# Key, value, output gate and z tiles of the first projection as pairs of half-size products

## What is computed

```python
hn = _rmsnorm(x, pre_g).astype(x.dtype)
proj = jnp.einsum('bld,de->ble', hn, w_in).astype(F32)          # 1024 -> 7176 features
q, k, v, og, ig, fg, z, xr, gr = _split(proj, EVEN_SPLITS)      # 1024 each; ig, fg: 4 each
kh = _heads(k, M_HEADS) * (M_DK ** -0.5)
li = (ig + b_i.astype(F32)).transpose(0, 2, 1)
lf = jax.nn.log_sigmoid(fg + b_f.astype(F32)).transpose(0, 2, 1)
...
hm = jax.nn.sigmoid(og) * hm
hm = _head_norm(hm, m_norm_g, M_HEADS) * jax.nn.silu(z)
```

## Time and profile before

| | us |
|---|---|
| median of 3 runs | 2317.79 (2316.91 to 2320.01) |
| profiled execution | 2318.86 |
| its span, first to last instruction | 2317.1 |
| mean granted clock of TensorE | 0.974 |
| VectorE busy / ScalarE busy / GpSimd busy | 1080.8 / 764.4 / 284.2 |

### The profile page before, as it was taken

One profiled execution on the slowest core, in us unless ns is written; L12 is line 12 of the kernel. 1 busy time (PEld: TensorE's weight loads), 2 busy tenths in 40 slices (PEclk: granted clock), 3 DMA queues, 4 the chain that ended last, 5 costly groups with the idle time before them and its releaser, 6 DMA issues. The chain is left out here.

```text
span 2317.1 us, 32021 instructions
## 1 busy us (share of the span) xinstructions
PE 2188.5 (94%) x12374; PEld 1898.7 (82%) x12374; DVE 1080.8 (47%) x1935; ACT 764.4 (33%) x1406; POOL 284.2 (12%) x287
## 2 busy tenths in 40 slices
PE   5999999999999799999986999999999799999998
PEld 4999999999999567767756999999999466666665
DVE  5455612121112565565535656755666654444442
ACT  5455512112221433333225444321232432222222
POOL 3010000000000111121113000000000332322232
PEclk8999999999999799999997999999999899999999
DMA  2122134333332644344313233344332544444442
GB/s 98 60 72 69 49 93 123 93 111 102 94 101 75 204 128 131 117 134 142 110 47 121 84 92 90 119 151 127 107 95 84 195 160 140 161 146 154 148 132 64
DMA packets 204453, 261.89 MB, mean 113 GB/s; under 512 B 47584, under 2 KB 151264, under 8 KB 202288
## 3 DMA queue, kind: packets, MB, share of 16 engines
q1 hardware_dynamic: 204336, 260.30, 35.7%
HBM read 170.29 MB, written 89.97 MB: 112 GB/s over the span
## 5 line engine op out<-in xcount | busy, mean ns | idle before, releaser
L361 PE MATMUL pa_ps<-a_XT_hi,pa_w_hi 128*128 128x358 f32 x1344 | 301.7, 333 | 0.3 <-PEq L196 0.3
L361 PE MATMUL pa_ps<-a_XT_hi,pa_w_lo 128*128 128x358 f32 x1344 | 293.9, 327 | 0.0
L361 PE MATMUL pa_ps<-a_XT_lo,pa_w_hi 128*128 128x358 f32 x1344 | 293.3, 326 | 0.0
L361 PEld LDWEIGHTS pa_ps<-a_XT_hi,pa_w_hi 128*128 128x128 f32 x1344 | 233.0, 189 | 5.9 <-issue 0.6
L361 PEld LDWEIGHTS pa_ps<-a_XT_hi,pa_w_lo 128*128 128x128 f32 x1344 | 232.2, 189 | 0.0
L361 PEld LDWEIGHTS pa_ps<-a_XT_lo,pa_w_hi 128*128 128x128 f32 x1344 | 231.6, 189 | 0.0
L345 DVE TENSOR_TENSOR pa_w_lo<-pa_w_raw,pa_w_hi 128x1024 fp32r<-128x1024 f32 x57 | 70.7, 1240 | 318.1 <-ACT pa_w_hi L341 315.8
L1833 DVE TENSOR_TENSOR pc_stage<-pc_ps,pc_stage 128x536 f32<-128x536 f32 x110 | 77.0, 712 | 105.0 <-PE pc_ps L1802 91.5
L954 PE MATMUL mc_ps<-mc_wout_hi,mc_mix_hi 128*128 128x512 f32 x288 | 118.9, 413 | 2.3 <-POOL mc_mix_lo L2753 1.4
L954 PE MATMUL ma_ps<-ma_wout_hi,ma_mix_hi 128*128 128x512 f32 x288 | 120.8, 419 | 0.0
L954 PE MATMUL ma_ps<-ma_wout_lo,ma_mix_hi 128*128 128x512 f32 x288 | 115.1, 400 | 0.0
(11 more groups left out here) (451 smaller groups left out, 4746.3 us busy)
## 6 DMA issues: line engine op xcount, KB each, us to landing
pa_w_raw<-in_w_a SPq DMA_DIRECT2D x57, 512.0 KB, 4.3
pc_w_raw<-in_w_c SPq DMA_DIRECT2D x49, 512.0 KB, 4.6
scr_c<-pc_stage SPq DMA_DIRECT2D x48, 512.0 KB, 3.2
scr_a<-pa_stage SPq DMA_DIRECT2D x40, 512.0 KB, 3.2
ma_hin<-scr_a SPq DMA_DIRECT2D x32, 512.0 KB, 3.7
mc_hin<-scr_c SPq DMA_DIRECT2D x32, 512.0 KB, 3.7
mc_sample_state<-in_s SPq DMA_DIRECT2D x32, 512.0 KB, 4.6
out_s_s<-mc_sample_state SPq DMA_DIRECT2D x32, 512.0 KB, 2.7
```

The costliest lines, as they stand in the source:

```text
L361: ins = pe.matmul(self.ps[:, 3 * s + t, 0:TC], w[:, k, :], x[:, k, t * TC:(t + 1) * TC], start=(k == 0 and j == 0), stop=(k == KT - 1 and ...
```

## The change

The k, v, og and z tiles of the first projection (32 tiles, from tile 25, `A_PAIRS0`, on) are made as 16 pairs with `HalfProducts`. The class moves ahead of `stage_project_a`, takes the number of its first tile, the scratch for the sums and the write semaphores as arguments, and takes in the methods that stood in `stage_project_c` (token sums, copies, additions). The q tiles stay as they are, written out instead of looped. Beside them run now: the gate rows (ScalarE at tile 0, VectorE at tiles 0 and 1, TensorE before tile 4, ScalarE's reading after tile 3), the token sums (tiles 2 to 5), and the weight sums of the first pair. The scaling of k, the sigmoid of og and z and the multiplication of z work in place on the staging tiles once the additions are through. The buffers of the channel recurrence are given back before those of the half products are taken; the gate rows lie in the space of the output weights, whose four loads are issued in pairs 1 to 4. In the second projection the calls are put in new places, with the same operations in the same order.

```diff
+A_PAIRS0 = 25
 # SP
+                for k in range(8):
+                    n, s = A_QKV0 + k, (1 + k) % 2
+                    if k < 6:
+                        G.load(sp, n + 2, s)
+                    else:
+                        HP.load(sp, 0, s)
+                    spill(stage_ready, k + 1, s, k // 2, k % 2)
...
+                sp.wait_ge(rows_ready, 1)
+                sp.dma_start(out_m, m_out[:]).then_inc(finished, 16)
+                for p in range(NPAIR):
+                    kind, h = kind_of(p)
+                    if p + 1 < NPAIR:
+                        for s in range(2):
+                            HP.load(sp, p + 1, s)
+                    if 1 <= p <= w_out.tiles // 2:
+                        sp.wait_ge(rows_turned, 1)
+                        sp.wait_ge(HP.t_ready, 1)
+                        w_out.load(sp, p - 1)
+                    for m in range(2):
+                        if kind == "v":
+                            spill(HP.added, HP.ready(p)[m], m, h, 4 + m)
+                        else:
+                            spill(final[m], tile_count(p), m, h, 2 * (1 + p // 4) + m)
 # ScalarE
+                for k in range(8):
+                    if k == 7:
+                        HP.split_lower_hi(act, 0)
+                        HP.split_upper_hi(act, 0)
+                    q_tile(k)
+                    if k == 0:
+                        gate_rows_act(act)
+                    if k == 2:
+                        act.wait_ge(lru_spilled, 32 * 8)
+                    if 2 <= k < 2 + KH:
+                        for i in range(2 * k - 4, 2 * k - 2):
+                            HP.t_his(act, i)
+                    if k == 3:
+                        gate_rows_act_out(act)
+                    if k == 6:
+                        HP.split_sums_hi(act, 0)
+                HP.t3_his(act)
...
+                    if kind == "k":
+                        act.activation(flat[m][:, 0:T], flat[m][:, 0:T], ACT.Copy, scale=0.0625).then_inc(final[m], 1)
+                    elif kind == "og":
+                        act.activation(flat[m][:, 0:T], flat[m][:, 0:T], ACT.Sigmoid).then_inc(final[m], 1)
                     else:
+                        act.wait_ge(z_read, 2 * h + m)
+                        act.activation(z_sig, flat[m][:, 0:T], ACT.Sigmoid).then_inc(sigmoid_ready, 1)
+                for p in range(NPAIR):
+                    more = p + 1 < NPAIR
+                    HP.copies(act, p, upper, lower)
+                    if more:
+                        HP.split_upper_hi(act, p + 1)
+                        HP.split_sums_hi(act, p + 1)
+                    finish(p, 0)
+                    if more:
+                        HP.split_lower_hi(act, p + 1)
+                    finish(p, 1)
 # VectorE
+                for k in range(6):
+                    G.split_lo(dve, A_QKV0 + 2 + k, (1 + k) % 2)
+                    if k < 2:
+                        gate_rows_dve(dve, k)
+                    else:
+                        for i in range(2 * k - 4, 2 * k - 2):
+                            HP.t_sums(dve, i)
+                            HP.t_lows(dve, i)
+                HP.sum_weights(dve, 0)
+                HP.t3_sum(dve, 0)
+                HP.t3_sum(dve, 1)
+                HP.split_sums_lo(dve, 0)
+                HP.split_lower_lo(dve, 0)
+                HP.split_upper_lo(dve, 0)
+                HP.t3_lows(dve)
...
+                for p in range(NPAIR):
+                    if p > 12:
+                        z_gate(p - 1, 1)
+                    HP.sums_of(dve, p, upper, lower, p + 1 < NPAIR, (lambda: z_gate(p, 0)) if p >= 12 else (lambda: None))
+                z_gate(NPAIR - 1, 1)
 # TensorE
+                for k in range(2, 8):
+                    if k == 4:
+                        gate_rows_pe(pe)
+                    n = A_QKV0 + k
+                    G.products(pe, n, (1 + k) % 2, n // 2, {})
+                pe.wait_ge(G.psum_free[1], A_PAIRS0 // 2)
+                pe.wait_ge(toks_read, 1)
+                for p in range(NPAIR):
+                    HP.products(pe, p)
```

The methods that these calls reach, as far as they are not those of the class before:

```diff
+    def copies(self, act, p, upper, lower):
+        if p == 0:
+            act.wait_ge(self.spilled[1], 32 * self.before)
+            self.copy(act, p, 5, lower[1])
+            self.copy(act, p, 4, lower[0])
+        act.wait_ge(self.spilled[0], 32 * (self.before + p))
+        self.copy(act, p, 1, upper[0])
+    def t_his(self, act, i):
+        k = i // 2
+        for m, (u, x) in enumerate(self.t_made(i)):
+            act.wait_ge(self.t_sum, 3 * k + i % 2 + m + 1)
+            act.activation(self.t_hi[u][:, k, :], x, ACT.Copy).then_inc(self.t_hi_ready, 1)
```

More of the change, by code:

```diff
@@ L414, in stage_project_a @@
         e_last = a.sb("pa_e_last", [4, 17])
+        temps = a.sb("pa_t_temps", [P, 3, HC])
+        lru = ExitStack()
+        la = make_alloc(nc, lru)
+        xe_p = la.sb("pa_xe_p", [P, 3 + NP_TOK])
+        xe_s = la.sb("pa_xe_s", [P, NSEQ, 3 + SLEN])
+        xc = la.sb("pa_xc", [P, TP])
+        gr_e = la.sb("pa_gate_r", [P, TP])
+        gi_e = la.sb("pa_gate_i", [P, TP])
+        av = la.sb("pa_decay", [P, T])
+        tv = la.sb("pa_tanh", [P, T])
+        lv = la.sb("pa_log", [P, T])
+        hv = la.sb("pa_h", [P, T])
+        silu = la.sb("pa_silu", [P, 3, TC])
+        sig = la.sb("pa_sigmoid", [P, 3, TC])
+        silu_f = silu[:].rearrange("p a b -> p (a b)")
+        lout = la.sb("pa_lru_out", [P, T])
+        lru_w = la.sb("pa_lru_w", [P, 2, P])
+        conv0 = la.sb("pa_conv0", [P, 8, NSEQ, 3])
+        h0 = la.sb("pa_h0", [P, 8, NSEQ])
+        lru.close()
+        room = w_out.rows[:].rearrange("p t d -> p (t d)")
+        gates, rows = room[:, 0:TP], room[:, TP:TP + T]
+        xf, ab, lf, bb, mm = (room[0:4, TP + (1 + k) * T:TP + (2 + k) * T] for k in range(5))
         sem = S.a.sem
@@ L445, in stage_project_a @@
         rows_turned = sem("pa_rows_turned")
+        toks_read = sem("pa_row_columns_read")
+        final = [sem(f"pa_{x}_tile_ready") for x in ("upper", "lower")]
+        z_read = sem("pa_z_sigmoid_read")
+        HP = HalfProducts(S, G, a, a, "pa", A_PAIRS0, tuple(temps[:, k, :] for k in range(3)) + (room[:, 7 * T + 2:7 * T + 2 + HC],), spilled, 4)
+        z_sig = temps[:].rearrange("p k t -> p (k t)")[:, 0:T]
         PROMPT = slice(0, NP_TOK)
@@ L457, in seqs, with kind_of, tile_count, halves @@
             return buf[:, NP_TOK:NP_TOK + NSEQ * SLEN].rearrange("p (s t) -> p s t", t=SLEN)
-        groups = ("q", "k", "v", "og", "z")
-        xf, ab, lf, bb, mm = (x[0:4, 0:T] for x in (gr_e, gi_e, av, tv, lv))
+        NPAIR = 16
+        def kind_of(p):
+            return ("k", "v", "og", "z")[p // 4], p % 4
+        def tile_count(p):
+            return p + 1 if p < 4 else p - 3
+        def halves(buf):
+            return [buf[:, m * HC:(m + 1) * HC].rearrange("p (a b) -> p a b", b=HC // 2) for m in range(2)]
+        upper, lower = halves(flat[0]), halves(flat[1])
         li = gates[0:4, 0:T]
@@ L496, in gate_rows_dve_0 @@
         def gate_rows_dve_0(dve, link):
-            link(dve.memset(rows[:], 0.0))
+            link(dve.memset(rows, 0.0))
             link(dve.memset(m_prev[:], 0.0))
@@ L699, in _ @@
-                for g in range(len(groups)):
-                    last = g == len(groups) - 1
-                    if g == 0:
-                        for d in range(2):
-                            tile(g, 0, d, False, True)
-                    with act.Fori(1 if g == 0 else 0, 3 if last else 4) as h:
-                        for d in range(2):
-                            tile(g, h, d, False, False)
-                    if last:
-                        for d in range(2):
-                            tile(g, 3, d, True, False)
-                    if g == 0:
-                        gate_rows_act(act)
-                    if g == 3:
-                        gate_rows_act_out(act)
+                    if k >= 2:
+                        act.wait_ge(spilled[s], 32 * (k // 2))
@@ L2012, in _ @@
                     g, h, d = head_of(p)
-                    if p == 0:
-                        act.wait_ge(spilled[1], 32 * 8)
-                        HP.copy(act, p, 5, lower[1])
-                        HP.copy(act, p, 4, lower[0])
-                    act.wait_ge(spilled[0], 32 * (8 + p))
-                    HP.copy(act, p, 1, upper[0])
+                    HP.copies(act, p, upper, lower)
                     if p + 1 < NPAIR:
@@ L2144, in _ @@
                 HP.split_upper_lo(dve, 0)
-                for k in range(KH):
-                    t3_low(k)
-                    if k + 2 < KH:
-                        t3_sum(k + 2)
+                HP.t3_lows(dve)
                 def gate(p, m, x):
```

567 lines of the change are left out of this document (254 added, 313 removed).

## The result

| | before | after |
|---|---|---|
| median, us (4 runs each) | 2318.9 (2316.91 to 2320.13) | 2282.0 (2279.99 to 2283.07) |
| profiled execution / its span | 2318.86 / 2317.1 | 2283.07 / 2281.3 |
| mean granted clock | 0.974 | 0.969 |

The ratio is 0.984 with a 95% interval of 0.982 to 0.985: faster by 37 us. Forecast were 2278, with a range of 2271 to 2288.

The account below looks back on a forecast made before the run. The prediction took the changed tiles to be bound by TensorE's matmuls alone. Its terms, -46.4 + 1.1 + 3.7 + 1.7 = -39.9 us, took 2318.86 to 2279.0, so a median of 2278 us, range 2271 to 2288.

Parts of the forecast that it names:

- The matmuls: Key, value, output gate and z tiles: 379.7 us removed, 16 pairs at 333.3 us added, a gain of 46.4 us.
- The end of the stage: Last product's read to next stage's first transfer: 7.09 us instead of 6.03, so +1.1 us for one more addition.
- The stall: Hand-over to the first pair: TensorE waits 3.7 us for split weight sums, 3.0 to 6.8 with the load's landing.
- The low clock: Behind the hand-over gap the granted clock drops to 0.50 for 3.4 us, costing 1.7 us.
- rival 2: Longer hand-over: load meets the query tile's write, takes 7.4 us, low clock lasts 6.8 us; 2283 us, chance 0.17.
- The query tiles: They take over gate rows and token sums at zero cost, with 4.6 us of cover behind the gate rows.
- Within the pairs: First projection's pairs cost nothing beyond the second layer's; tightest cover 5.8 us, for the copy of product 1.
- the twin: Second layer's projection, already run as pairs of seven half-size products at 123.7 ns a matmul; most prices come from it.
- The second layer: Its code is only rearranged, so its cost was put at zero.
- the sum: All terms together, -39.9 us against the profiled execution of 2318.86 us, giving 2279.0 us.
- Rival 1: Shorter hand-over: the load lands early and the clock is not lowered; 2275.5 us, chance 0.12.
- Rival 4: Slower than before: matmul pace follows the number of weight loads instead of the columns; 2386 us, chance 0.03.

## Why the prediction was right, and where it was not

1. **The matmuls.** Forecast 333.3 us for 16 pairs at 123.7 ns. Measured from the first product to the reading of the last: 711.28 - 376.62 = 334.7, less 1.6 for the clock = 333.0, which the run with the early load, without a low clock, shows by itself. The run with eight products prices a matmul at 123.7 ns by itself. Right, and shown.
2. **The end of the stage.** Forecast 7.09 us; measured 718.47 - 711.28 = 7.19.
3. **The stall.** Forecast 3.7; measured 3.91. The chain was the one worked out (load, weight sums, two token sums, low part): taking the load out of it removed the stall, and taking the token sums out of it removed 2.7 us. Step by step from the end of tile 6 (360.84): load on its way at +2.6 us, landed at +7.0, weight sums at +9.5, token sums at +13.8, low part done at +15.5, as forecast. What the prediction did not see is the second wait right behind it, that of the fifth product for ScalarE's copy: it shows only when the first is shortened alone.
4. **The low clock.** Forecast 1.7, half of a drop of 3.4 us; measured a drop of 3.4 us, and 1.6 us less in the pairs where it is gone. The size rested on one row. In the run with 8 late copies and in that with 210 columns, at stalls of 4.0 and 3.6 us, the drop was rival 2's 6.8.
5. **The query tiles.** Forecast zero with 4.6 us of cover behind the gate rows; measured zero, with 4.5 us (307.0 to 311.5), and the added clears were paid from exactly there. VectorE was through with the last token sums 11.7 us into their tile (348.97 to 360.66); 11.8 were forecast.
6. **Within the pairs.** Forecast zero, with 5.8 us as the tightest cover; measured zero. The 5.8 us hold for the last three pairs (about 6 us). But the middle pairs have 8.1, and the tightest place is pair 1 with 4.3, which the prediction missed: in the twin that copy had ended 4.3 us into the pair, here the write of pair 0 holds it to 7.6. It cost nothing, so the zero was right, but in pair 1 with less room than stated. Taking 5.8 for every pair made the forecast for 14 copies twice too large.
7. **The second layer.** Costed at zero, and wrong: +1.0 in its norm and projection and +2.5 in its mixing, both repeated in the second traces. The 3 us of range for drops in the mixing stages covered it, and drops they are, but the prediction took them for scatter around zero. Against the 2279.0 of the sum the profiled execution took 2283.07: of these 4.1 us 3.5 are the second layer, 0.7 the two stages around the first projection, and the first projection is 0.1 better than forecast.
8. **Rival 1 and 2** (2275.5 and 2283). The measured time lies near rival 2's, but neither of its mechanisms happened: the stall was 3.9 and the low clock 3.4 us. The time alone would have told the wrong story.
9. **Rival 4.** The pace by weight loads. Not at 268 columns, but a floor exists: it begins near 230 to 241 columns (an estimate), at 106 to 111 ns, well under the 138.8 from which the change would have lost. The Trainium skill (TensorE: Matmul & The Clock Gate, Back-to-back issue gap), from which the prediction had 81 ns for 128 columns and 131 ns for 512, is not borne out here: the line through both gives 82 ns for 134 columns and 99 for 268, estimates, and 134 columns took 212.8 ns at clock 0.50, 106 by halving, and 268 took 123.7. Nor does its N / 2.4 + 2.5, which it calls the gap of an isolated matmul, describe this stream: it gives 90 ns for 210 columns and 114 for 268, estimates, where 111.2 and 123.7 were measured.

## What to carry to other kernels

Where a stretch is bound by TensorE alone and a twin of the new form already runs in the kernel, the twin's pace times the count gives the gain to a microsecond; what is left to work out is the hand-over, instruction by instruction on each queue, and the gaps' cost in clock on top of their length. Compare stages, not whole times: the stage that was changed repeated within 0.1 us here, while unchanged stages behind it moved by 2.5. Cutting matmuls into smaller ones pays only while they are above the floor, some 230 to 240 columns for this data by the estimate above; the scheme applied a second time would fall under it. Mend a stall at the first link of its chain, for a shortcut in the middle may only uncover the next wait.

## What the runs showed of the hardware

- A floor under float32 matmuls that each load their own 128x128 weights: 213 ns at clock 0.50 with 134 and with 170 columns, 163 ns at 0.65 with 170; at 1.00 it is at most the 111 ns of 210 columns.
- At clock 0.50 a matmul of 268 columns took about 223 ns, at 1.00 123.7.
- Behind a stall of 3.5 to 4.0 us and in front of matmuls of 134 or 170 columns the clock stayed at 0.50 for 1164 and 594 us, to the end of the pairs and a little beyond, although TensorE shows as busy throughout. In front of 210 or 268 columns it came back after 3.4 or 6.8 us. Whether the stall is needed for it stays open.
- Gaps on TensorE in this stage and what followed. 0.80, 0.96 (in nine pairs), 1.20, 1.51 and 1.91 us: nothing. 2.6, 2.68 and 3.03: 3.4 us at 0.50. 2.91: 6.8. Of the seven stalls of 3.5 to 4.0 us at the hand-over in front of 210 or 268 columns five were followed by 3.4 us and two (one of 3.6, one of 4.0) by 6.8. 4.66 and 6.65 us: 5.0 and 5.9 us at 0.50 behind their end. In the last stage 3.24 us: nothing in one kernel and 3.4 us in the other. The length of the gap alone doesn't decide it.
- The same pairs of the second layer ran 0.35% slower in every changed kernel at clock 1.00, with TensorE full; the cause is not known.
